# A transformer layer with 32 routed experts: token slots from one-hot matmuls, raw rows in the gather, spare rows skipped

## What is computed

```
h = x + token_mixer(rms_norm(x, g_attn_norm)) 
y = h + hier_moe(rms_norm(h, g_ffn_norm))
hier_moe: group g = top 1 of 4 (softmax of x @ w_group_router + bias)
          two experts = top 2 of the 8 in that group (softmax of x @ w_expert_router + bias)
          gate = g_val * e_val / sum(e_val)
          y += gate * ((silu(x @ w_gate[e]) * (x @ w_up[e])) @ w_down[e])      256 hidden, 32 experts
```

## Time and profile before

| | us |
|---|---|
| median of 3 runs (644.75 to 645.97) | 645.04 |
| the profiled execution | 643.67 |
| its span, first to last instruction | 642.0 |
| PE busy in it | 530.8 (83%) |
| DVE busy | 223.6 (35%) |
| ACT busy | 147.0 (23%) |
| POOL busy | 133.2 (21%) |
| DMA in the chain that ended last | 45% |
| PE in that chain | 25% |

### The profile page before, as it was taken

How to read it: one execution, slowest core, us unless ns; L and a number is a source line. 1 busy time by engine, 2 the same in 40 slices (tenths; PEclk the granted TensorE clock), 3 DMA queues, 4 the chain that set the end, 5 groups by cost and what they waited for, 6 DMA issues and landing times.

```text
span 642.0 us, 8839 instructions
## 1 busy us (share of the span) xinstructions
PE 530.8 (83%) x3092; PEld 373.3 (58%) x3093; DVE 223.6 (35%) x602; ACT 147.0 (23%) x310; POOL 133.2 (21%) x200
## 2 busy tenths in 40 slices
PE   5889999997898989999725877989788897777762
PEld 4768988884444568888624545555445564434430
DVE  4743335225959562566650211121211211111110
ACT  6734343322546221121201101010100100000000
POOL 0122232032244000034323102111201232011110
PEclk9999999999999999999856989799989999889997
DMA  8730100000620039243467999999999999999992
GB/s 333 240 142 35 32 2 1 1 0 1 236 72 27 2 137 387 100 132 133 171 227 253 405 374 388 392 367 379 388 393 390 392 392 379 403 390 392 388 363 34
DMA packets 31163, 148.81 MB, mean 232 GB/s; under 512 B 7139, under 2 KB 7798, under 8 KB 18822
## 3 DMA queue, kind: packets, MB, share of 16 engines
q1 hardware_dynamic: 25376, 128.60, 50.2%
q0 software_dynamic: 5712, 19.72, 11.7%
q10 hardware_dynamic: 38, 0.01, 0.0%
HBM read 132.48 MB, written 17.00 MB: 233 GB/s over the span
## 4 chain that ended last, share of the span: by engine, by line
DMA 45%; PE 25%; issue 10%; DVE 6%; POOL 4%; ACT 1%; POOLq 0%; SPq 0%
DMA expert_w<-in_w_down 25%; DMA expert_w<-in_w_up 19%; PE ps L476 4%; PE ps L477 4%; PE ps L481 4%; PE ps L641 3%; POOL slot_tokens L1390 2%; PE ps L582 2%; DVE p_sb L1130 2%; PE ps L596 2%; PE ps L599 1%; PE ps L628 1%; PE ps L516 1%; DMA g_rows<-token_rows,idx_now 1%; PE ps L667 1%
## 5 line engine op out<-in xcount | busy, mean ns | idle before, releaser
L767 PE MATMUL ps<-expert_w,xT 128*64 128x256 f32 x1152 | 132.2, 386 | 16.4 <-DMA expert_w<-in_w_up 6.8
L767 PEld LDWEIGHTS ps<-expert_w,xT 128*64 128x64 f32 x1152 | 97.7, 140 | 55.5 <-issue 27.8
L783 PE MATMUL ps<-expert_w,hT 128*64 128x512 f32 x288 | 76.8, 681 | 23.7 <-DMA expert_w<-in_w_down 13.2
L1432 POOL DMA_INDIRECT out<-y_sb,idx_now x18 | 28.7, 1593 | 202.6 <-DVE y_sb L1302 201.8
L783 PEld LDWEIGHTS ps<-expert_w,hT 128*64 128x64 f32 x288 | 25.5, 155 | 63.1 <-issue 60.7
L1290 DVE SCALAR_TENSOR_TENSOR hid<-s_act,gate,ps 128x256 f32<-128x256 f32 x18 | 11.9, 660 | 141.5 <-ACT s_act L968 141.5
L476 PE MATMUL ps<-w_in_hi,aT_hi 128*128 128x384 f32 (+2 forms) x120 | 43.7, 368 | 0.0
L1302 DVE COPY y_sb<-ps 128x512 f32<-128x512 f32 x18 | 12.5, 692 | 89.5 <-PE ps L783 89.5
L477 PE MATMUL ps<-w_in_lo,aT_hi 128*128 128x384 f32 (+2 forms) x120 | 40.8, 344 | 0.0
L968 ACT ACTIVATE s_act<-ps 128x256 f32<-128x256 f32 x18 | 6.9, 384 | 133.7 <-PE ps L767 133.7
L973 ACT ACTIVATE y_sb<-ps 128x512 f32<-128x512 f32 x18 | 10.8, 597 | 105.6 <-PE ps L783 105.6
(11 more groups left out here) (205 smaller groups left out, 856.5 us busy)
## 6 DMA issues: line engine op xcount, KB each, us to landing
expert_w<-in_w_gate SPq DMA_DIRECT2D x32, 1024.0 KB, 9.7
expert_w<-in_w_up SPq DMA_DIRECT2D x32, 1024.0 KB, 8.5
expert_w<-in_w_down SPq DMA_DIRECT2D x32, 1024.0 KB, 10.4
w_in_raw<-in_w_in SPq DMA_DIRECT2D x8, 608.0 KB, 10.3
w_out_raw<-in_w_out SPq DMA_DIRECT2D x8, 512.0 KB, 3.6
token_rows<-rows SPq DMA_DIRECT2D x6, 528.0 KB, 3.4
out<-h_sb SPq DMA_DIRECT2D x6, 512.0 KB, 2.9
x_sb<-in_x_prompt SPq DMA_DIRECT2D x4, 512.0 KB, 9.9
```

Source lines behind the costliest of these rows:

```text
L767: mm = pe.matmul(ps[r, 2, g * FH:(g + 1) * FH], xT[:, q.o, k, r], w_gu(b, lane, k, g), start=(k == 0), stop=(k == KD - 1))
L783: mm = pe.matmul(ps[r, 4 + half, :], hT[:, q.o, k, r], w_dn(b, lane, k, half), start=(k == 0), stop=(k == 1))
L1432: pool.indirect_dma_start(out=out, out_offset=bass.IndirectOffsetOnAxis(ap=idx, axis=0), in_=y_sb[:, buf, :], in_offset=None, compute_op=A ...
```

## The change

1. **Slots by matmul.** For each tile VectorE makes `slot_a`, one-hot rows of the slot (0 to 127) that each of a token's two choices has in its pair (`slot_of`), and ScalarE makes `slot_b`: the one-hot expert mask times token number, times gate, and times the norm factor (3 x 32 columns). TensorE multiplies and accumulates them over all tiles in PSUM bank 5 (`slots`, 2 matmuls of 96 columns a tile). From this VectorE writes `idx_all` and the gates and norm factors of all pairs (`gate_all`). The scatter to `slot_tokens` stays for the extra passes; its last tile, the reload `idx_more` and all of this now stand behind the first two gathers on POOL's queue.
2. **Raw rows.** The table `token_rows` holds `h_sb` itself (1,024 floats, no spare rows), stored from ScalarE's queue; gates and norm factor go to a second table for the extra passes. The router's gain is multiplied into `w_router` at the start; logits are scaled by the norm factor afterwards; `second_norm` goes. After a gather, the gain `g_x` is applied in `x_copy` (ScalarE: four operations of 128 columns for one of 512), the norm factor in `silu` and in the gate. The transposes of gathered rows read every eighth column.
3. **Bound.** Gathers and adds carry `bounds_check=T - 1`: rows of empty slots (number 768 and up) are to be skipped.
4. **Order.** TensorE interleaves half tiles; SP loads all of pair 1 right after the last `out` store and then waits for the first gather ahead of pair 2. Five small loads and two table fills move from SP's to POOL's queue, ahead of POOL's first statistics.

Cut to its core:

```diff
-    table = nc.dram_tensor("token_rows", [T + P, ROW], F32, kind="Internal").ap()
+    table = nc.dram_tensor("token_rows", [T, D], F32, kind="Internal").ap()
+    gate_table = nc.dram_tensor("token_gates", [T, E + 1], F32, kind="Internal").ap()
...
-                else:
-                    load_pair(sp, 1, 1, range(3))
-                if i >= 1:
-                    store_rows(i - 1)
-            load_pair(sp, 1, 1, range(3, 4))
...
-            store_rows(NT - 1)
-            sp.wait_ge(slots_stored, 2 * NT * 16)
+            load_pair(sp, 1, 1)
+            sp.wait_ge(main.gathered[0], 16)
+            load_pair(sp, 2, 2)
             sp.wait_ge(counts_done, 1)
...
+            def slots(i):
+
+                pe.wait_ge(slot_a_done, i + 1)
+                pe.wait_ge(slot_b_done, 3 * (i + 1))
+                for c in range(2):
+                    mm = pe.matmul(ps[:, 5, 0:3 * E], slot_a[:, c, :], slot_b[:, c, :, :].rearrange("t n e -> t (n e)"), start=(i == 0 and c == 0),
+                                   stop=(i == NT - 1 and c == 1))
+                mm.then_inc(slot_mm, 1)
...
             for i in range(NT):
-                out_half(i, 0)
-                if i >= 1:
-                    row_transposes(i - 1)
-                out_half(i, 1)
+                out_part(i, 0, False)
+                if i >= 1:
+                    h_transposes(i - 1, 1)
+                out_part(i, 0, True)
+                if i >= 1:
+                    logits(i - 1, 0)
+                    logits(i - 1, 1)
                 if i >= 2:
-                    ranks(i - 2)
-                if i >= 1:
-                    logits(i - 1)
-            row_transposes(NT - 1)
-            ranks(NT - 2)
-            logits(NT - 1)
+                    slots(i - 2)
+                out_part(i, 1, False)
+                h_transposes(i, 0)
+                out_part(i, 1, True)
+                if i >= 1:
+                    ranks(i - 1)
+            logits(NT - 1, 0)
+            h_transposes(NT - 1, 1)
+            logits(NT - 1, 1)
+            slots(NT - 2)
             ranks(NT - 1)
+            slots(NT - 1)
...
+                blocks = src.rearrange("t (p k) -> t k p", k=KD)
                 for k in range(KD):
-                    mm = pe.transpose(ps[:, banks + k // 4, (k % 4) * P:(k % 4 + 1) * P], src[:, k * P:(k + 1) * P], ident)
+                    mm = pe.transpose(ps[:, banks + k // 4, (k % 4) * P:(k % 4 + 1) * P], blocks[:, k, :], ident)
...
+            def slot_gates(i):
+                act.wait_ge(mask_done, i + 1)
+                if i >= 1:
+                    act.wait_ge(slot_mm, i)
+                slot_part(i, 2, lambda c: 404 + i)
+                act.wait_ge(wts_done, i + 1)
+                slot_part(i, 1, lambda c: 410 + c)
+
+            def slot_values(i):
+                act.wait_ge(val_done, i + 1)
+                slot_part(i, 0, lambda c: 396 + c)
...
-                act.activation(xT[:, q.o, 0:4, :], ps[:, bank, :].rearrange("p (k t) -> p k t", k=4), ACT.Copy).then_inc(q.x_act, 1)
-
-            def silu(q, n):
+                for k in range(4):
+                    ins = act.activation(xT[:, q.o, k, :], ps[:, bank, k * P:(k + 1) * P], ACT.Copy, scale=g_x[:, k:k + 1])
+                ins.then_inc(q.x_act, 1)
...
+                for c in range(2):
+                    ins = dve.tensor_tensor_reduce(out=RF[:, 320 + E * c:320 + E * (c + 1)], in0=RF[:, 224 + E * c:224 + E * (c + 1)],
+                                                   in1=rank, scale=1.0, scalar=0.0, op0=ALU.mult, op1=ALU.add,
+                                                   accum_out=RF[:, 390 + c:391 + c])
+                step(ins)
+                step(dve.tensor_scalar(RF[:, 392:394], RF[:, 390:392], float(LANE), 1024.0, ALU.is_ge, ALU.mult))
+                step(dve.scalar_tensor_tensor(out=RF[:, 394:396], in0=RF[:, 390:392], scalar=RF[:, 188:189], in1=RF[:, 392:394],
+                                              op0=ALU.add, op1=ALU.add))
+                dve.tensor_scalar(RF[:, 396:398], RF[:, 394:396], -1.0, consts[:, C_TOK + i:C_TOK + i + 1],
+                                  ALU.mult, ALU.add).then_inc(val_done, 1)
+                if i >= 1:
+                    dve.wait_ge(slot_mm, i)
+                dve.tensor_scalar(slot_a[:, 0, :], iota_slot, RF[:, 394:395], None, ALU.is_equal)
+                dve.tensor_scalar(slot_a[:, 1, :], iota_slot, RF[:, 395:396], None, ALU.is_equal).then_inc(slot_a_done, 1)
...
+            dve.wait_ge(slot_mm, NT)
+            for lane in range(2):
+                r = slice(lane * LANE, (lane + 1) * LANE)
+                dve.tensor_scalar(idx_all[r, 0:PAIRS], ps[r, 5, PAIRS * lane:PAIRS * (lane + 1)], spare_row[r], None,
+                                  ALU.add).then_inc(idx_done, 1)
+            dve.tensor_copy(idx_all[:, PAIRS:], spare_row).then_inc(idx_done, 1)
...
+            with nc.allow_non_contiguous_dma(reason="short rows"):
+                for dst, src in ((tok_ids[:, :], a["tokens"]),
+                                 (w_router[:, :, 0:EG], a["w_group_router"][0].rearrange("(k p) n -> p k n", k=KD)),
+                                 (w_router[:, :, EG:], a["w_expert_router"][0].rearrange("(k p) n -> p k n", k=KD)),
+                                 (g_router[:, :], a["g_ffn_norm"][0].rearrange("(k p) -> p k", k=KD)),
+                                 (g_x[:, :], a["g_ffn_norm"][0].rearrange("(p k) -> p k", k=KD))):
+                    pool.dma_start(dst, src).then_inc(router_in, 16)
+            pool.dma_start(slot_table.rearrange("(a b) c -> a (b c)", a=P),
+                           a["slots"].rearrange("(a b) c -> a (b c)", a=P)).then_inc(setup_dram, 16)
+            pool.dma_start(out[T:T + P, :], a["zeros"]).then_inc(setup_dram, 16)
+            step(pool.memset(neg_half[:, :], -0.5))
...
-            def gather(dst, idx, done):
-                pool.indirect_dma_start(out=dst, out_offset=None, in_=table,
-                                        in_offset=bass.IndirectOffsetOnAxis(ap=idx, axis=0)).then_inc(done, 16)
+            def gather(dst, src, idx, done):
+                pool.indirect_dma_start(out=dst, out_offset=None, in_=src, in_offset=bass.IndirectOffsetOnAxis(ap=idx, axis=0),
+                                        bounds_check=T - 1, oob_is_err=False).then_inc(done, 16)
...
                 pool.indirect_dma_start(out=out, out_offset=bass.IndirectOffsetOnAxis(ap=idx, axis=0),
-                                        in_=y_sb[:, buf, :], in_offset=None, compute_op=ALU.add).then_inc(q.added, 16)
+                                        in_=y_sb[:, buf, :], in_offset=None, compute_op=ALU.add,
+                                        bounds_check=T - 1, oob_is_err=False).then_inc(q.added, 16)
...
-            gather_pair(0, 0, 1)
-            pool.wait_ge(idx_rest_in, 32)
+                return 2 * PAIRS - 1 if isinstance(j, int) and j == PAIRS - 1 else 2 * j + 2
+
+            gather(g_rows[:, 0, :], table, idx_all[:, 0:1], main.gathered[0])
+            gather(g_rows[:, 1, :], table, idx_all[:, 1:2], main.gathered[1])
+            pool.wait_ge(h_stored, 16 * NT)
+            fill_slots(NT - 1)
+            pool.wait_ge(slots_stored, 2 * NT * 16)
+            pool.dma_start(idx_more[:, :], slot_table[BLOCK:2 * BLOCK, :].rearrange("(s j) c -> s (j c)", j=PAIRS)).then_inc(idx_rest_in, 16)
+            pool.wait_ge(counts_done, 1)
+            pool.wait_ge(gates_stored, 16 * NT)
+            pool.wait_ge(idx_rest_in, 16)
             first_more_gather(0)
-            gather_pair(1, 1, 2)
             run_pairs(pool, pair)
```

More of the change, by code:

```diff
@@ L42 @@
 BLOCK = 2 * LANE * PAIRS
-ROW = D + E
 N_VEC = KD + KQ + KKV + 2 + NG
@@ L1324, in pair @@
                 more_passes(j, again)
-            dve.wait_ge(main.gathered[0], 16)
-            gates(main, g_rows[:, 0, :], 0, 0, 0)
+            gates(0, 0)
             x_copy(main, 0)
```

379 lines of the change are left out of this document (208 added, 171 removed).

## The result

| | us |
|---|---|
| before, median | 645.02 |
| the changed kernel, median of 4 runs (649.8 to 651.66) | 650.49 |
| ratio, with its 95% interval | 1.0071 (1.0042 to 1.0099) |
| span of the profiled execution, before and after | 642.0 and 648.8 |
| forecast | 634, range 618 to 644 |

A forecast was written before the change was run, and what follows sets the result against it. The prediction took the expert stage's weight stream, with all 16 DMA engines full, as the bound. Its terms, 0 at the start, -2.7 for an earlier stream and -8 within it, gave -10.7 us: 634 us, range 618 to 644.

The forecast's parts named there:

- From the gather to pair 3: 0.9 us lost: First gather's landing to the stream's start: pair 0's two passes take 28.5 us, not 27.4; restart after idle engines costs 2.0.
- Start: 0: Kernel start: moving seven loads to POOL's queue nets 0, with ends of 2.7 us gained and 3 us lost.
- the upper end: Kernel start: 3 us lost, since the moved transfers stand among the early weights on which both engines wait.
- The rival of a late POOL: Kernel start: slow POOL issues bring its statistics 14.6 us late and TensorE waits, total 649 us; chance 0.1.
- Output projection: +4.4: Until the last h_sb half: slot matmuls 2.0 us, tile 4's logits 1.9 and tile 5's transposes 0.5 come ahead.
- To the first gather: Last h_sb store to the first gather's issue: 11.8 us instead of 24.2; landing 8.7 us later under load.
- Transposes that read every eighth element: 0: Transposes of gathered rows on TensorE: strided reads cost nothing; if their time doubled, the total would be 2.2 us higher.
- Stream: -8: Weight stream of pairs 3 to 15: skipping unfilled rows in gathers and adds saves 8 us, from 0 to 22.
- a fixed deal: Expert stream: each DMA engine serves the same rows of every DMA, so full low slots save little; 634 us, chance 0.55.
- a DMA share below 1: Expert stream: sign of the likeliest case, together with 18.9 to 19.1 us a pair.
- The rival of an even deal: Expert stream: skipped rows spread over all 16 DMA engines, saving 22 us, total 620 us; chance 0.2.
- Tail: 0: Last weights to the end of the kernel: stays 15.7 us.

The follow-up runs named there:

- both other orders of slots: Changed kernel with each lane's slots dealt bit-reversed: 641.75 us, 0.9944 of before; or, within each half, four neighbours holding slots 8 apart: 636.26 us, 0.9831.
- the order by halves behind an unbroken start: Changed kernel with half of pair 1 held until idx_more lands, seven loads on SP's queue, slots dealt 8 apart within lane halves: 619.25 us, 0.961 of before.
- the hold: Changed kernel with half of pair 1's loads held until the reload idx_more has landed: 639.83 us, 0.9907 of before; measured again, 641.08 us, 0.9947.

## Why the prediction was wrong

**The step that failed: "From the gather to pair 3: 0.9 us lost".** It priced pair 0's two passes by TensorE's and ScalarE's work, 28.5 us, and took for granted that the extra rows are there. They measured 35.3, 7.9 more than before: 3.6 of it is the wait for the rows, 3.8 the lower clock behind it (0.9 in the transposes, 2.9 in the products), and only the remaining half microsecond lies in the rest of both passes. The trace of before hid the question, since the gather of `more_rows` was issued there 2 us behind the first, long before its use. The change puts four things ahead of it on POOL's queue (a second gather, the scatter of tile 5, its landing and the reload), and puts pair 1's 6 MB on the engines beside them. The forecast priced just this load for the first gather (8.7 us; 9.3 measured) and not for the next DMAs in line. It named pair 0's second pass as what pair 3 waits for, and even wrote that the engines would stand idle before pair 3's issue, without asking when the rows of that pass arrive. The two runs without the pass price the error: 15.6 us against 4.9.

Point by point, the span missed its forecast by 17.5 us (-10.7 against +6.8): start 2.8, output projection 1.9, from there to the first gather's landing 0.7, this step 6.8, stream 4.0, tail 2.3, less 1.0 because the stream's restart behind the gates took 1.0 us and not 2.0.

**Start: 0.** Measured +2.8 at the output projection. The moved transfers delayed the early weights, as the upper end had it, but by 5.4 us with the clock and not by 3. The 2.7 us of idle time went, and so the sum came out near the upper end of 3, partly by luck; 0 was no middle. Whether the sooner loads did anything in the changed kernel isn't shown, since a TensorE that is 5.4 us late would have covered the same waits. POOL itself was not late: its first statistics stand at 6.78 us against 5.66. The rival of a late POOL had the right sign and the wrong mechanism.

**Output projection: +4.4.** Measured 6.3 (9.1 less the start's 2.8). The tile period went from 13.75 to 14.26 us, as worked out (4 slot passes, 0.5). The forecast gives no number for a product of `logits`; it is two passes of 0.12 us, from the 16 in 1.95 us of the earlier trace rows. The forecast missed a wait of the second tile:

```profile
262.05 0.66 PE L698 MATMUL ps<-consts_sb,h_sb 128*128 128x128 f32 x4 [1.63 <-DVE h_sb L1230]
```

`x_res`, issued at 251.08, takes 10.2 us beside pair 0's weights. TensorE now transposes `h_sb` in the same tile and so sees it land.

**To the first gather.** 11.9 us against 11.8 forecast, landing after 9.3 against 8.7: right. The gather was later than forecast (344.5, not 339.1) by what went before.

**Transposes that read every eighth element: 0.** Right. At full clock eight take 1.16 us, where blocks in order take 1.09. The Trainium skill's rule ("SBUF — State Buffer", "SBUF: two separate sides"), by which the forecast would have been 2.2 us higher, doesn't show on TensorE here.

**Stream: -8.** Measured -4.0. The mechanism was right: a fixed deal keeps most of the skipped rows' time (20 us of POOL's DMA time were saved, 4 arrived), and both other orders of slots bring it back. The size was off: 6.5 was the worked-out value and I went up to 8. Counted from pair 3's gates it is -5.2. The sign given for it, "a DMA share below 1", is wrong: the share stays 1 and the weight packets grow longer. The rival of an even deal, 22 us at most, came near what an even order is worth; the order by halves behind an unbroken start shows 235.7 - 217.0 = 18.7. Some of that is where the count starts, since the hold issues pair 3's `w_up` 4.0 us behind the gates: from the gates it is 237.9 - 221.0 = 16.9.

**Tail: 0.** 2.3 us longer from pair 15's `w_up` issue. 1.7 of it is the last down products at the lower clock:

```profile
630.38 5.35 PE L791 MATMUL ps<-expert_w,hT 128*64 128x512 f32 x16 [2.09 <-DMA expert_w<-in_w_down]
```

The earlier trace rows has 3.67 there. But the kernel before without its pass shows 6.37 as well, and from pair 15's `w_up` issue to the end the other two traces of the kernel before, without the pass and with the bound, take 36.7 and 36.2 us against 36.4 here. So the 34.0 of the profiled kernel before was a short one, and this is no effect of the change.

## What to carry to other kernels

When a wait is taken away, follow the next instruction that the freed resource depends on, with every DMA on its way, and price each of them under the load that the change itself brings forward; here one row in an extra pass cost more than the whole change saved. Rows skipped in an indirect DMA save time only as far as they are spread evenly over the DMA engines: order the slots so that each engine's share is alike. Plain loads moved to another queue may still delay the weights that everybody waits for, since all queues share the engines: here `w_uq` landed 2.9 us later.

## What was not expected of the hardware

- A small indirect scatter lands 3.0 us after its issue on nearly idle DMA engines and 11.0 beside 1 MB weight loads; the reload of a small table, 1.9 against 5.6.
- After 3.59 us without work TensorE ran 64 products at half clock for most of their 10.0 us; after 0.61 us it ran them in 7.13. In four other traces waits of 1.22, 2.36, 3.08 and 3.92 us were followed by 8.8, 9.0, 8.9 and 9.7. A wait of 3 us thus cost 6.7 with the transposes (3.0 + 0.8 + 2.9).
- An uneven deal of rows over the DMA engines doesn't lower their busy share. It shows in the time that the other queue's packets take: 2.51 us per MB against 2.42, with the same median and a longer tail.
